# A transformer kernel on one core: where ScalarE waits for a broadcast load, and which engine adds a mask to a table

## The reference, cut to what matters

```python
h = modulate(x, n_mix, sh1, sc1)          # rmsnorm(x) * g * (1 + scale) + shift
cq, ckv, kr, nq, nk, nv = split_cols(h @ w_in, sizes)      # layer 1 of the first network
bias = rpb[:, key_row - r + (NA_ROWS - 1)][:, :, dc_idx]   # bias of the neighbourhood attention
s_win = einsum(q, k_w) * scale + bias                      # only keys of the window
```

## Time and profile before

| | us |
|---|---|
| median of 3 runs | 2477.07 (2473.58 to 2483.8) |
| the profiled execution, its own time | 2477.24 |
| its span, first to last instruction | 2475.5 |
| TensorE busy | 2264.4 |
| VectorE busy | 1846.7 |
| ScalarE busy | 1472.1 |
| GpSimd busy | 14.9 |

### The profile page before, as it was taken

How to read it: one execution, slowest core, us unless ns; L and a number is a source line. 1 busy time by engine, 2 the same in 40 slices (tenths; PEclk the granted TensorE clock), 3 DMA queues, 4 the chain that set the end, 5 groups by cost and what they waited for, 6 DMA issues and landing times. The chain is left out here.

```text
span 2475.5 us, 54570 instructions
## 1 busy us (share of the span) xinstructions
PE 2264.4 (91%) x21226; PEld 1795.2 (73%) x21249; DVE 1846.7 (75%) x2407; ACT 1472.1 (59%) x1947; POOL 14.9 (1%) x12
## 2 busy tenths in 40 slices
PE   5988999998978789999999998989999999999997
PEld 3744789896844469977699786777777777777775
DVE  3267577777336767756677657699999999999998
ACT  3136466664113556553466534588888888888885
POOL 0000000002000000000000000000000000000000
PEclk8979999999978999998999998999999999999999
DMA  7350377775457047754587753399999999999996
GB/s 309 136 221 1 128 272 270 282 278 188 146 218 287 1 159 291 266 193 168 196 289 277 257 203 131 117 379 416 412 411 419 417 418 417 418 418 407 418 417 246
DMA packets 121212, 674.38 MB, mean 272 GB/s; under 512 B 13488, under 2 KB 13968, under 8 KB 67088
## 3 DMA queue, kind: packets, MB, share of 16 engines
q1 hardware_dynamic: 120032, 664.47, 69.2%
q10 hardware_dynamic: 1072, 8.42, 0.8%
HBM read 671.79 MB, written 1.05 MB: 272 GB/s over the span
## 5 line engine op out<-in xcount | busy, mean ns | idle before, releaser
L1182 PE MATMUL ps<-projected_halves,weights_halves 128*128 128x256 f32 x1504 | 364.8, 283 | 0.0
L1182 PEld LDWEIGHTS ps<-projected_halves,weights_halves 128*128 128x128 f32 x1504 | 288.3, 192 | 3.2
L1503 DVE TENSOR_TENSOR aux<-weights,aux 128x1024 bf16<-128x1024 f32 x223 | 271.3, 1217 | 0.7 <-ACT aux L1452 0.6
L1164 DVE SCALAR_TENSOR_TENSOR weights_halves<-normed_or_mix_halves,weights 128x1024 fp32r<-128x1024 f32 (+1 forms) x145 | 222.2, 1537 | 62.8 <-ACT normed_or_mix_halves L1161 62.8
L1498 DVE TENSOR_TENSOR turned<-weights,turned 128x2048 bf16<-128x2048 f32 x112 | 256.4, 2289 | 13.4 <-ACT turned L1446 8.4
L1446 ACT ACTIVATE turned<-weights 128x2048 bf16<-128x2048 f32 x112 | 213.7, 1908 | 61.4 <-DMA weights<-moe 58.1
L1383 PE MATMUL ps<-projected,turned 128*128 (+1 forms) x1792 | 232.9, 206 | 0.0
L1384 PE MATMUL ps<-projected,turned 128*128 (+1 forms) x1792 | 232.9, 206 | 0.0
L1385 PE MATMUL ps<-projected,turned 128*128 (+1 forms) x1792 | 232.9, 206 | 0.0
L1452 ACT ACTIVATE aux<-weights 128x1024 bf16<-128x1024 f32 x223 | 232.0, 1041 | 1.1 <-PE ps L1397 1.1
L837 PE MATMUL ps<-weights_halves,normed_or_mix_halves 128*128 128x512 f32 (+4 forms) x576 | 218.4, 379 | 0.0
(11 more groups left out here) (380 smaller groups left out, 5755.5 us busy)
## 6 DMA issues: line engine op xcount, KB each, us to landing
weights<-moe SPq DMA_DIRECT2D x224, 1024.0 KB, 8.6
weights<-moe SPq DMA_DIRECT2D x224, 512.0 KB, 6.7
weights<-l_ffn SPq DMA_DIRECT2D x66, 1024.0 KB, 4.8
weights<-ada SPq DMA_DIRECT2D x64, 1024.0 KB, 5.6
weights<-l_ffn SPq DMA_DIRECT2D x66, 512.0 KB, 4.6
weights<-ada SPq DMA_DIRECT2D x64, 512.0 KB, 5.9
weights<-ffn SPq DMA_DIRECT2D x28, 1024.0 KB, 4.8
weights<-w_in SPq DMA_DIRECT2D x24, 948.0 KB, 4.7
```

Source lines behind the costliest of these rows:

```text
L1164: return dve.scalar_tensor_tensor(out=to, in0=lead.bitcast(F32), scalar=-LEAD, in1=src, op0=ALU.mult, op1=ALU.add)
L1182: mm = pe.matmul(out_, ring(RINGR, j, t, t + PB), h_rest[:, k, :], start=False, stop=(k == KD - 1))
L1503: dve.tensor_tensor(down4[j % SLOTS][1], RING[:, slot(j), 2 * D:3 * D], down4[j % SLOTS][0], ALU.subtract).then_inc(back_used.sem, 1)
```

## The change

ScalarE's wait for the row parameters leaves `modulate` and stands at the end of ScalarE's list in the `split_linear` behind it, in the three places. The load itself is issued where it was. The mask is added by VectorE: after the blocks of each of the groups 0 to 3 have been copied out, VectorE adds it for two heads, with the same eight instructions in all. Before the first two it waits for the loads. GpSimd has nothing left to do in that block.

```diff
@@ modulate, ScalarE
                 keep_odd(KD)
-                if rows is not None and not begin:
-                    act.wait_ge(rows_in.sem, rows_in.at(16))
@@ split_linear
-            if beside is not None:
-                @block.gpsimd
-                def _(pool):
-                    beside(pool)
-
@@ split_linear, ScalarE, behind all its pieces
+                if rows:
+                    act.wait_ge(rows_in.sem, rows_in.at(16))
@@ split_linear, VectorE, in the loop over the groups
                     for j in range(early, last + 1):
                         keep_block(i, j)
+                    if beside is not None:
+                        beside(dve, i)
@@ layer 1
-    def mask_bias(pool):
-        pool.wait_ge(const_in.sem, 96)
-        for h in range(8):
+    def mask_bias(dve, i):
+        if i == 0:
+            dve.wait_ge(const_in.sem, 96)
+        for h in range(2 * i, 2 * i + 2) if i < 4 else ():
             o = AUX[:, h * 512:(h + 1) * 512]
-            pool.tensor_tensor(o, o, EX[:, 4608:5120], ALU.add)
+            dve.tensor_tensor(o, o, EX[:, 4608:5120], ALU.add)
```

More of the change, by code:

```diff
@@ L714, in modulate @@
         S.hop_b.done(1)
-        if rows is not None and not begin:
-            rows_in.done(16)
     def turn(src, tiles, nb, dst, scale=None):
@@ L773, in split_linear @@
     def split_linear(toks, h_hi, h_lo, room, cols, blocks, store, src=None, beside=None, gates=(), nb=0, turned=None,
-                     residual=None):
+                     residual=None, rows=False):
         a, first, per_group = place.n, 2 * len(gates), KD // 2
@@ L908, in _ @@
                         keep_block(i, j)
+                    if beside is not None:
+                        beside(dve, i)
+        if rows:
+            rows_in.done(16)
         if gates:
@@ L1908, in build @@
              loads=((AUX[:, :], d["na_bias"]), (EX[:, 4608:5120], d["na_mask"])))
-    def mask_bias(pool):
-        pool.wait_ge(const_in.sem, 96)
-        for h in range(8):
+    def mask_bias(dve, i):
+        if i == 0:
+            dve.wait_ge(const_in.sem, 96)
+        for h in range(2 * i, 2 * i + 2) if i < 4 else ():
             o = AUX[:, h * 512:(h + 1) * 512]
-            pool.tensor_tensor(o, o, EX[:, 4608:5120], ALU.add)
+            dve.tensor_tensor(o, o, EX[:, 4608:5120], ALU.add)
     split_linear(512, all_tokens(XNR), all_tokens(HTR), EXR[:, 0:4608], groups_of("l1_w_in"),
-                 lambda c0: range(4) if c0 >= CKV else range(2), keep(p1), src=ht, beside=mask_bias)
+                 lambda c0: range(4) if c0 >= CKV else range(2), keep(p1), src=ht, beside=mask_bias, rows=True)
     lat = XN[:, 0:2, :].rearrange("p a b -> p (a b)")
@@ L2375, in build @@
         split_linear(T, own_tokens(XNR), own_tokens(HTR), EXR[:, :], groups_of("w_in"), lambda c0: range(2), store2,
-                     src=lambda k: HT[:, k, 0:T], turned=(turn_conv, keep_conv))
+                     src=lambda k: HT[:, k, 0:T], turned=(turn_conv, keep_conv), rows=True)
         S.turned.done(3)
```

## The result

The changed kernel took 2453.38 us, median of 4 runs (2446.86 to 2455.17), against 2479.34 us of 4 runs of the kernel before on the same chip: a ratio of 0.9906 with an interval of 0.989 to 0.9922. A second measurement, against 17 runs of the kernel before, gave 2453.11 against 2474.49 us, a ratio of 0.9907 (0.989 to 0.9924). The forecast was 2463.2 us in a range that ended at 2458.5. It was the right direction, and some 7 to 12 us too little. The ratios are taken over all runs and are not the quotients of the two medians (0.9907 of 2474.49 would be a gain of 23.0 us). The 26 us rest on 4 runs of the kernel before; its 54 later ones have medians of 2473.8 to 2474.5, so 21 is the better figure for the gain. By the same medians the prediction started some 3 us too high, at 2477.2.

The account below looks back on a forecast made before the run. TensorE was taken as the bound, held up by row-parameter loads at three block ends and by VectorE slowed beside GpSimd in layer 1. Waits 7.0 plus GpSimd's adds 7.0 made 14.0 us: 2477.2 to 2463.2 us, range 2458.5 to 2470.5.

Parts of the forecast that it names:

- the wait in layer 1: Layer 1's block end: without the wait for row parameters the next block starts at 594.74, not 598.36: 3.6 us won.
- GpSimd's adds: Layer 1, group 0 of the projections: without GpSimd's adds VectorE runs as in the first layer; 7.0 us won.
- VectorE's adds at nothing: Behind groups 0 to 3 of layer 1: eight mask adds on VectorE are covered; 0 us, upper bound 5.5.
- the wait in its new place at nothing: ScalarE's end in split_linear, three places: loads land tens of microseconds before the wait; cost zero.
- Rivals A: Only the moved waits pay; another wait or slow VectorE replaces GpSimd's slowdown in group 0: 2470.2 us, chance 0.08.
- B: VectorE's mask adds are exposed behind the groups: 2468.7 us at worst, 2464.6 if only group 0's pair shows; chance 0.10.
- D: Second network: TensorE's zeros, not ScalarE's wait, hold the block ends; 1.5 + 1.9 us missing, 2466.6 us, chance 0.03.
- the price of the second network's two waits: Second network's two block ends: moving the waits wins 1.5 us in the first layer and 1.9 in the second.
- moves forward as a whole: Behind the three places, work ordered by releases and semaphores shifts earlier together; no stage gives the 14.0 us back.
- part 1 of the change: The wait leaves modulate at three block ends; each boundary then costs 0.35 us behind the last engine; 7.0 us won together.
- rival C: TensorE's clock stays at its lower level for groups 0 to 2 of layer 1: 41 us lost, 2504 us, chance 0.03.

Follow-up runs that it names:

- wait_only: Kernel before with ScalarE's three waits moved as in the change, GpSimd's mask adds left as they were: 2462.49 us, ratio 0.9952.
- mask_only: Kernel before with the mask adds moved from GpSimd to VectorE, the three waits left in place: 2466.80 us, ratio 0.9971.
- layer1_only: The change in layer 1 of the first network alone, with its mask; second network as in the kernel before: 2463.06 us, ratio 0.9956.
- gap_filled: Kernel before with waits kept and TensorE's idling at the three block ends filled with 16 or 8 more zero products: 2471.86 us, ratio 0.9996.
- second_only: Kernel before with the wait moved only in the second network's two layers; layer 1 and its mask unchanged: 2464.92 us, ratio 0.9965.
- heads_held: Changed kernel with 3 or 10 zero products added behind the modulation rows in layer 1's two head norms: 2455.68 us, ratio 0.9925.
- later_6: Changed kernel with six more zero products at the block end ahead of the projections in each second-network layer: 2459.97 us, ratio 0.9946.
- later_12: Changed kernel with twelve more zero products at the block end ahead of the projections in each second-network layer: 2461.41 us, ratio 0.9950.
- short_tail: Changed kernel with three zero products in place of six at the second network's two block ends: 2456.72 us, ratio 0.9930.
- before_scan: Kernel before with eleven zero products under TensorE's 2.65 us of idling in each second-network scan stage: 2471.46 us, ratio 0.9992.

## Why the prediction was wrong, step by step

**Right: the wait in layer 1.** 3.6 us in the sum, 3.6 in every trace in which it was moved, 11.4 - 7.7 = 3.7 in the medians (each of the two uncertain by 3 to 4 us). The load that landed last was read from the earlier trace rows, and TensorE's zeros were next in line, as forecast.

**Right: GpSimd's adds.** 7.0 in the sum, 6.9 in the traces, 7.7 in the medians. Group 0 took 11.00 us; the low parts took 0.64 us each and, with GpSimd beside them in wait_only, 1.73. The rule of the Trainium skill that the prediction named ("SBUF — State Buffer", "Who interferes with whom") agrees with that pair, 0.64 and 1.73 us, but these runs don't tell it from shared bandwidth either.

**Right: VectorE's adds at nothing, and the wait in its new place at nothing.** From group 1 on the kernels are alike to 0.01 us. Rivals A, B and D are refuted: group 0 has no gap, no pair of adds shows, and the second network's block ends did move.

**Wrong: the price of the second network's two waits, and with it that behind the three places the work "moves forward as a whole".** The sum had 1.5 + 1.9 = 3.4 us; the runs show 8.9 and 10.0. In parts:

- The block ends themselves: the five kernels that kept these waits lie on average 0.5 us above and 0.2 below the first profile (the load took 7.6 to 8.4 us to land in them); those with moved waits at -1.4 and -2.5. That is 1.9 + 2.3 = 4.2 us. I read a number that scatters from a single trace.
- The clock behind the idling: in 3 of these 10 block ends group 0 came out 0.8 to 0.9 us longer, never with the wait moved. Some 0.5 us for both layers together.
- The scans. Of the four kernels that kept the waits and left the stage as it is (before, mask_only, layer1_only, gap_filled), 5 of 8 stages were long; of the five that moved them and changed nothing else behind (both profiles of the changed kernel, wait_only, second_only, heads_held), none of 10. At 3.65 and 3.77 us that is an average of some 4.6 us. The 3 short ones among the 8 are just those in which the clock had fallen behind the block end: each of the 8 paid either 0.9 us there or 3.7 in its scan.

Together 9.3 us, between the two measurements; the first part is read from traces of each kernel, the other two are averages over few of them. With the layer-1 terms it makes 19.9 us for the whole change, where 21.4 were measured with an interval from 18.8 to 27.2. The rest of the 9.8 us between the forecast time and the measured one is the starting point, some 3 us too high.

Two steps failed. In part 1 of the change the two waits were priced from one trace at 3.4 us, where the block ends gave 4.2. The larger one is the clock: rival C had it only as a possible loss in layer 1, and the sum put a gain from it at nothing, where the traces show some 5.1 us (0.5 + 4.6). The row that should have warned me is in the same trace: the kernel before ran its scan stages at 0.50 for twelve microseconds with TensorE busy in 11.78 of them, behind 2.65 us of idling. A kernel whose clock is low in several stages can win from a shift in time as well as lose, and such a stage belongs in the range on both sides.

The Trainium skill ("TensorE: Matmul & The Clock Gate", Part 1) says that how many products run on the low clock varies from run to run, advises against fitting their number, and puts the penalty under 1% of a typical span. This case does not test that figure: the 7.4 us, 0.3% of the span, are the price of two stages, while a mean granted clock of 0.964 puts some 180 us of the kernel before at the lower level, and no run shows what all of them cost. But 7.4 us are over half of what the change's own places gave, and 5 of 8 against none of 10 speaks against pure chance, though the stages of one trace are not independent and the count leaves out the kernels that disturb them: with the waits moved and zero products added or taken away, later_6 had a long one, later_12 two and short_tail two of other lengths.

**What stays open.** Why a block end that comes 1.4 to 2.5 us earlier should keep the stage short; that the moved wait causes it is argued from the counts. In the traces what differs is the moment of the fall, counted from the first ScalarE instruction of the stage of decays and scans (1135.02 us in the first layer before): in 6 stages it comes 8.6 to 9.4 us behind it and the low stretch lasts 13.6 us, in 14 it comes at 9.9 to 10.9 us and lasts 3.4, at 7.8 to 7.9 (later_12, and short_tail's first layer) 6.8. short_tail's second layer, at 11.0 with 10.2 us, does not fit a simple order. later_6 and later_12 were to test this by their medians and could not tell. Each kernel but the changed one has one trace, so whether a stage's form is the same in every execution of a kernel isn't shown; 5 of 8 is a count over kernels. The granted clocks of all executions point the same way: 0.9709 on average over 20 with the second network's waits moved (the changed kernel, wait_only, second_only), 0.9676 over 54 of the kernel before, 0.9679 over 29 of mask_only, layer1_only and gap_filled. The first difference is an estimated 16 us less at the lower level, where the counts of long stages and of falls behind a block end would give 15. And the surplus of the scans is shown in traces, while the medians only fit it: before_scan's interval holds zero.

## What to carry to other kernels

Where a profile shows stages with TensorE busy at a granted clock of 0.50, count them, and put their price on both sides of the range of a change that shifts what runs ahead of them; here it was 85 us ahead. But find out first whether the time hangs on them: heads_held raised the clock and won nothing. Take the length of a wait for a load from several traces or from the spread of its landings, not from one. Filling idling with zero products did no good here: of four kernels that did it, none won more than its measurement is uncertain.

## What the hardware showed that was not expected

- TensorE's clock, fallen to the lower of its two levels in or behind 2.65 us of idling, stayed there for 3.4, 6.8, 10.2 or 13.6 us in otherwise equal stages, with TensorE busy from the end of the idling on. Over the 24 stages of the twelve traces without extra zero products in that stage, those in which the clock fell at nearly the same moment had the same length; why is open.
- The same eight products of 128x128 in fp32 took 1.09 us or 1.97 us at the two levels. The 12 products of 128x3 in front of them took 1.50 us at the full level and 2.38 where the clock fell 0.4 us after their start.
- One boundary between two blocks costs TensorE 0.30 us when nobody is late. It was 0.30 in all of the changed kernel's three places.
- The load of 1280 KB in 128 partitions took 11.2 to 11.7 us from issue to landing in layer 1 of the first network and 7.6 to 9.2 in the second network, over fourteen traces.
